# Latent attention of a hybrid diffusion block: blocks of 1024 queries, query halves in column tiles, denominators inverted in four pieces

## The reference, cut to what matters

```python
def attend(q, k, v):
    s = jnp.einsum('bqhgd,bkhd->bhgqk', q, k, preferred_element_type=jnp.float32) * (HEAD_DIM ** -0.5)
    p = jax.nn.softmax(s, axis=-1).astype(v.dtype)
    return jnp.einsum('bhgqk,bkhd->bqhgd', p, v)
```

## Time and profile before

| | |
|---|---|
| Median of three runs | 3813.49 us (3811.07 to 3816.92) |
| Profiled execution | 3814.73 us, its span 3813.1 us |
| Busy over the span | PE 93%, DVE 58%, ACT 34%, POOL 39% |
| Stage that is changed | 762 to 1894 us, 30% of the span |

### The profile page before, as it was taken

How to read it: one execution, slowest core, us unless ns; L and a number is a source line. 1 busy time by engine, 2 the same in 40 slices (tenths; PEclk the granted TensorE clock), 3 DMA queues, 4 the chain that set the end, 5 groups by cost and what they waited for, 6 DMA issues and landing times. The chain is left out here.

```text
span 3813.1 us, 51191 instructions
## 1 busy us (share of the span) xinstructions
PE 3534.7 (93%) x17340; PEld 2666.5 (70%) x17340; DVE 2207.0 (58%) x3467; ACT 1283.1 (34%) x2070; POOL 1494.8 (39%) x991
## 2 busy tenths in 40 slices
PE   6999996799999999999769959999999998999798
PEld 4787883456666666666468847888998886887586
DVE  4666644566666666666346655443334443777576
ACT  3422334334444444444320034222223332664300
POOL 1133313456777777677623321100000001444354
PEclk8999997789999999999979979999999999999899
DMA  5234537411111111111155442221211114677563
GB/s 189 95 113 131 141 94 233 132 38 34 34 34 33 39 37 33 34 34 33 44 190 176 138 136 97 78 71 66 73 57 57 47 36 131 207 220 242 210 210 137
DMA packets 313681, 394.25 MB, mean 103 GB/s; under 512 B 81965, under 2 KB 208061, under 8 KB 313361
## 3 DMA queue, kind: packets, MB, share of 16 engines
q1 hardware_dynamic: 281312, 317.34, 27.3%
q10 hardware_dynamic: 21040, 37.43, 3.1%
q0 software_dynamic: 11136, 36.98, 2.4%
HBM read 267.99 MB, written 121.20 MB: 102 GB/s over the span
## 5 line engine op out<-in xcount | busy, mean ns | idle before, releaser
L1403 DVE TENSOR_REDUCE al_mx<-al_sx 128x1 f32<-128x512 f32 (+1 forms) x960 | 562.6, 632 | 267.9 <-PE al_sx L1480 254.7
L235 PE MATMUL pj_acc<-pj_whi,pj_h_hi 128*128 128x512 f32 x1808 | 711.6, 394 | 0.0
L236 PE MATMUL pj_acc<-pj_wlo,pj_h_hi 128*128 128x512 f32 x1808 | 706.0, 390 | 0.0
L237 PE MATMUL pj_acc<-pj_whi,pj_h_lo 128*128 128x512 f32 x1808 | 705.5, 390 | 0.0
L1343 ACT ACTIVATE al_e<-al_st 128x1024 f32<-128x1024 f32 x432 | 443.2, 1027 | 577.5 <-PE al_st L1493 568.0
L845 DVE TENSOR_TENSOR pj_h_lo<-pj_hall,pj_h_hi 128x1024 fp32r<-128x1024 f32 x258 | 377.8, 1465 | 282.4 <-ACT pj_h_hi L713 282.3
L1373 POOL TENSOR_TENSOR al_acc_p<-al_acc_p,al_e 128x1024 f32<-128x1024 f32 x192 | 457.5, 2383 | 20.1 <-POOL al_acc_p L1369 0.4
L787 POOL TENSOR_TENSOR pj_wlo<-pj_wst,pj_whi 128x2048 fp32r<-128x2048 f32 x28 | 129.0, 4606 | 728.0 <-ACT pj_whi L697 728.0
L713 ACT ACTIVATE pj_h_hi<-pj_hall 128x1024 fp32r<-128x1024 f32 x258 | 270.5, 1055 | 415.2 <-PE pj_acc L237 397.4
L1502 PE MATMUL al_acc<-al_e,vres 128*64 128x512 f32 x1728 | 402.5, 601 | 0.0
L235 PEld LDWEIGHTS pj_acc<-pj_whi,pj_h_hi 128*128 128x128 f32 x1808 | 341.5, 189 | 70.1 <-issue 0.6
(11 more groups left out here) (285 smaller groups left out, 5731.8 us busy)
## 6 DMA issues: line engine op xcount, KB each, us to landing
s_proj<-pj_stage SPq DMA_DIRECT2D x162, 256.0 KB, 2.0
pj_wst<-in_w ACTq DMA_DIRECT2D x28, 1024.0 KB, 5.5
ml_k<-s_proj SPq DMA_DIRECT2D x36, 512.0 KB, 4.4
ml_v<-s_proj SPq DMA_DIRECT2D x36, 512.0 KB, 8.6
mo_in<-s_proj SPq DMA_DIRECT2D x34, 512.0 KB, 6.2
hm_w<-in_ada_w SPq DMA_DIRECT2D x16, 1024.0 KB, 8.7
ml_qt<-s_qt SPq DMA_DIRECT2D x32, 512.0 KB, 6.1
s_h<-ml_h POOLq DMA_DIRECT2D x32, 512.0 KB, 8.0
```

The costliest lines, as they stand in the source:

```text
L235: nc.tensor.matmul(out, s_hi, m_hi, start=start, stop=False)
L236: nc.tensor.matmul(out, s_hi, m_lo, start=False, stop=False)
L237: return nc.tensor.matmul(out, s_lo, m_hi, start=False, stop=stop)
L1403: V.tensor_reduce(mx[:, x:x + 1], slots[x % NSX][:, 0:spans[x % NS][1]], AX.X, ALU.max).then_inc(sx_max, 1)
```

## The change

The stage gets a function of its own, `latent_attention`, unrolled (no hardware loop). `attention` stays for the context. A block is now 1024 queries of one head; there are 24.

- Key tiles are taken singly, `NP = 18`, with the two query halves side by side: `st` holds 128 keys x 1024 queries. The two value matmuls of a step now share the value tile, and the two column tiles are the two query halves. Nothing has to be folded: `acc` holds 64 rows for each half.
- The denominators come from a matmul with `ones` of 128x64 as the stationary operand, so each arrives copied on 64 partitions, in the layout of `acc` (`denominators`, before key tile 7). ACT copies them out of PSUM into `den`. DVE inverts them in place in four pieces of 128x128 at key tiles 8 to 11, and multiplies by `ot` at tile 13 (`norm`). PE turns the product by four transposes at tile 14, and ACT copies the result out for the store.
- The sums: DVE adds tiles 0, 1, 3, 9, 10, 12, POOL all others and the two parts together. `asum` is 128x1024; the add of the two halves is gone.
- 40 maxima per block. The places 20 and 38 of the slot order are taken by the denominators and the transposes. There are three maxima before key tiles 1 and 4, and none before 16 and 17.
- The bias of the next block is done at key tile 15 of 18, and its row goes out in eight DMAs.

```diff
@@ -1562,6 +1562,333 @@
                 values(NKV - 1, n, n, 0)
                 folded(n - 1, n - 1)
                 folded(n, n)
+
+
+def latent_attention(nc, m, a, s, keep, kres, vres):
...
+    NP, HALVES = NT, 2
+    BLOCKS = LT * P // (HALVES * CH)
+    TOTAL = NQ * BLOCKS
+    W = HALVES * CH
+    QT = W // P
...
+    DEN_AT, TURN_AT, NSX = 20, 38, 3
+    AHEAD, EXTRA = (2, 3, 2, 2, 3) + (2,) * 10 + (0, 0, 0), 2
+    DEN_J, PIECES_J, ON_J, TURN_J, BIAS_J = 7, (8, 9, 10, 11), 13, 14, 15
+    ADD_D, ADD_P = (1, 3, 9, 10, 12), (5, 4, 6, 7, 8, 11, 13, 14, 15, 16, 17)
...
+    turn = [("max", x) for x in range(NX)]
+    turn.insert(DEN_AT, ("den", 0))
+    turn.insert(TURN_AT, ("turn", 0))
...
+    def items(n):
+
+        at = 0
+        out = []
+        for j in range(NP):
+            extra = EXTRA if j and j % C == 0 else 0
+            out.append((range(at, at + extra), range(at + extra, at + extra + AHEAD[j])))
+            at += extra + AHEAD[j]
...
+            def row(n):
+                sp.wait_ge(negm_done, n + 1)
+                if n == 0:
+                    sp.wait_ge(zero_done, 1)
+                for i in range(QT):
+                    sp.dma_start(qb[HD:HD + 1, n % 2, i * P:(i + 1) * P].bitcast(F32), negm[:, n % 2, i:i + 1].bitcast(F32)).then_inc(row_ld[n % 2], 16)
+
+            def store(n):
+                sp.wait_ge(o_done, n + 1)
+                for b in range(HALVES):
+                    rows = s["attn"][tokens(n), head(n) * HD:(head(n) + 1) * HD][b * CH:(b + 1) * CH]
+                    sp.dma_start(rows.rearrange("(t p) d -> p t d", p=P), o[:, n % 2, :, b, :]).then_inc(stored[n % 2], 16)
+
+            for n in range(2):
+                load_x(n)
+                load(n)
+            row(0)
+            for n in range(TOTAL):
+                if n + 2 < TOTAL:
+
+                    sp.wait_ge(sx_mm, (n + 1) * NX)
+                    load_x(n + 2)
+                if n:
+                    store(n - 1)
+                if n + 1 < TOTAL:
+                    row(n + 1)
+                if n + 2 < TOTAL:
+
+                    sp.wait_ge(st_mm, (n + 1) * NP)
+                    load(n + 2)
+            store(TOTAL - 1)
...
+            def denominators(n, slot):
+                act.wait_ge(den_mm, n + 1)
+                if n:
+                    act.wait_ge(on_done, n)
+                nc.scalar.activation(den[:], slots[slot][:], ACT.Copy).then_inc(den_out, 1)
+
+            def result(n, slot):
+                act.wait_ge(turn_mm, n + 1)
+                if n >= 2:
+                    act.wait_ge(stored[n % 2], 16 * HALVES * (n // 2))
+                nc.scalar.activation(o[:, n % 2].rearrange("p t b d -> p (t b d)"), slots[slot][:], ACT.Copy).then_inc(o_done, 1)
...
+                    if j == DEN_J and n:
+                        denominators(n - 1, DEN_AT % NSX)
+                    if j == TURN_J and n:
+                        result(n - 1, TURN_AT % NSX)
+                    weights(n, j)
...
+                if n >= 2:
+                    pool.wait_ge(den_mm, n - 1)
+                nc.gpsimd.tensor_tensor(asum[:, n % 2], acc_p[:], acc_d[:], ALU.add).then_inc(asum_done, 1)
...
+            def inverse(n, i):
+                dve.wait_ge(den_out, n + 1)
+                V.reciprocal(den[:, i * P:(i + 1) * P], den[:, i * P:(i + 1) * P]).then_inc(rden_done, 1)
+
+            def norm(n):
+                dve.wait_ge(rden_done, CH // P * (n + 1))
+                dve.wait_ge(ot_done, n + 1)
+                if n:
+                    dve.wait_ge(turn_mm, n)
+                V.tensor_tensor(on[:], ot[:, n % 2, :], den[:], ALU.mult).then_inc(on_done, 1)
...
+            adds = {3: (0,), 6: (1,), 12: (2, 3), 15: (4,)}
+            for n in range(TOTAL):
+                for j, (extra, ahead) in enumerate(items(n)):
+                    some(extra)
+                    for i in adds.get(j, ()):
+                        add(n, i)
+                    if j == ON_J and n:
+                        norm(n - 1)
+                    some(ahead)
+                    if j in PIECES_J and n:
+                        inverse(n - 1, PIECES_J.index(j))
+                    if j == BIAS_J and n + 1 < TOTAL:
+                        bias(n + 1)
+            for i in range(CH // P):
+                inverse(TOTAL - 1, i)
+            norm(TOTAL - 1)
...
+                for b in range(HALVES):
+                    cols = slice(b * CH, (b + 1) * CH)
+                    mm(st[k % 2][:, b], kres[:, g, keys], qa[:, p, cols], start=True, stop=False)
+                    y = mm(st[k % 2][:, b], kres[:, NKV + g, keys], qb[:, p, cols], start=False, stop=True)
+                y.then_inc(st_mm, 1)
...
+                for b in range(HALVES):
+                    y = mm(acc[b * HD:(b + 1) * HD], vres[:, j, group_of(n), :], e[:, k % RING, b], start=(j == 0), stop=(j == NP - 1))
+                y.then_inc(pv_mm, 1)
...
+                for b in range(HALVES):
+                    y = mm(slots[slot][b * HD:(b + 1) * HD], ones[:], asum[:, n % 2, b], start=True, stop=True)
+                y.then_inc(den_mm, 1)
...
+                for i in range(CH // P):
+                    y = nc.tensor.transpose(slots[slot][:, i * P:(i + 1) * P], on[:, i * P:(i + 1) * P], keep["ident"][:])
+                y.then_inc(turn_mm, 1)
...
+                    if j == 0 and n:
+                        for i in range(NP - C, NP):
+                            values(n - 1, i)
+                    if j and j % C == 0:
+                        some(extra)
+                        for i in range(j - C, j):
+                            values(n, i)
+                    some(ahead)
+                    scores(n, j)
...
@@ -2372,7 +2699,7 @@
     m.end()
     attention(nc, m, a, s, keep, kres, vres, "ac_", 0, CT, 1, CT)
     m.end()
-    attention(nc, m, a, s, keep, kres, vres, "al_", CT, 4, LT // 4, NT)
+    latent_attention(nc, m, a, s, keep, kres, vres)
     m.end()
     attention_stack.close()
     out_weights = OutWeights(nc, m, 0, a["w_out0"], 2)
```

175 lines of the change are left out of this document (added).

## The result

The changed kernel takes 3865.13 us (median of 4, 3863.35 to 3867.61) against 3814.71 us before (median of 4, 3811.07 to 3816.92): 1.0128 times as long, 95% interval 1.0115 to 1.0141. The forecast was 3851 us. The span of the profiled execution grew by 51.1 us, from 3813.1 to 3864.2 us. Of that, 43.5 us lie before the end of the stage (1894.4 to 1937.8 us) and 7.6 us after it, in code that the change does not touch.

What follows compares the result with a forecast made beforehand. PE was taken as the bound, busy 1100.9 of 1102.9 us. A block: 43.97 + 2.3 + 0.46 + 0.3 + 0.1 = 47.1 us against 45.96; with the stage's ends +38, so 3813.5 + 38 = 3851 us, range 3795 to 3885.

Steps and rivals of the forecast that it cites:

- PE's own work and the small waits: Per 1024 queries: PE's work falls from 45.96 to 43.97 us; waits 0.46 (tile 17), 0.3 (slots, place 41), 0.1 (bias row).
- The reciprocal: DVE's inversion of 128x128, four per block: 0.94 us each, from a slope of 6 ns per column.
- The race: Key tiles 8 to 13: DVE needs 15.8 us, PE 13.6, so PE waits 2.3 us per block for maxima.
- place 37: Matmul in the slot order at key tile 13, waiting for the maximum of place 34: a 1.5 us wait.
- DVE's hole: After place 25 the next matmul for DVE comes only after the values: about 1.5 us no order can use.
- POOL's hold: At key tile 12 DVE's adds stand until POOL's add of tile 11 ends: about 0.65 us.
- B: Rival: DVE keeps up if a reciprocal costs 0.3 us; block 44.6, 3794 us; chance 0.18.
- C: Rival: waits half as large, smaller hole or holds; block 45.6 to 46.0, 3817 to 3826, down to 3806; chance 0.12.
- rival D: DVE meets POOL's full 2.4 us at tile 12 (3892), or is passed over before the row (3906); chance 0.15.
- The row: Next block's bias row, eight DMAs on SP: there 9.7 us after place 41, PE at 9.6; costs 0.1 us.
- The scores of tile 17: No maxima between tiles 15, 16, 17, so these scores wait for the exponentials of 15: 0.46 us.
- The ends of the stage: First scores at 793.0 us, last values end at 1917.3, stage end at 1932.3 against 1894.4: +38 us.

Runs made afterwards that it cites:

- DVE out of the way: Changed kernel with each reciprocal on 1 column and POOL's running adds on 128 of 1024 columns, work left out: 3802.5 us, a block of 45.07.
- The first experiment, the small reciprocals: Changed kernel with each of the four reciprocals per block on 1 column instead of 128: 3854.6 us, ratio 1.0104.
- the ninth DMA: Changed kernel with one more DMA of 128 values ahead of the eight of the bias row: 3877.9 us, ratio 1.0162.
- the version with the transposes there: The swapped and late version with transposes between the scores of tiles 16 and 17: 3962.4 us; with bias ahead of add and row ahead of stores, 3795.5.
- the swapped and late version: Changed kernel, POOL adding tile 9 and DVE tile 11, reciprocals and product behind the bias, transposes in the next block: 3813.2 us, ratio 1.0000.

## Why the prediction was right, and where not

**PE's own work and the small waits.** Summed without the race they were 43.97 + 0.46 + 0.3 + 0.1 = 44.83 us. Measured with DVE out of the way: 45.07, or 45.0 without the long first block. Right to 0.2 us. The transposes cost 0.44 instead of 0.5 us (0.35 from 1304.16 to 1304.51, 0.09 behind them). The pass of ones cost 1.21 instead of 1.11 (1.01 in the lines below, 0.20 around it); I had it at the price of a pair of value matmuls. What is left of the 0.2 us I can't place.

```profile
1332.14 1.08 PE L1856 MATMUL al_sx<-al_asum,al_ones 128*64 128x512 f32 x4
1333.15 0.50 PE L1827 MATMUL al_sx<-kres,al_qx 128*128 128x512 f32 x1
```

**The reciprocal.** 943 ns against 0.94 us: the slope of the earlier trace rows carried over from 4 columns to 128. The estimate of about 1.2 us that I had made from the Trainium skill ("VectorE: DVE Perf Modes", First, the fixed hardware budget) does not hold here: 943 ns were measured, and the 25 us that hung on it did not come.

**The race.** Forecast: PE waits 2.3 us, in two small pieces at tiles 11 and 12 and 1.5 us at place 37. Measured: 0.3, 0.3 and 1.5 us. By the experiments 2.33 us per block. From place 22 to place 37 PE took 15.80 us (1334.41 to 1350.21), as forecast, and DVE's hole was 1.63 us against 1.5. POOL's hold was 0.7 us against 0.65, but that was partly luck. I gave no working for it and said that POOL had just begun on tile 11; in fact it was 1.6 us into an add of 2.35 us.

**What failed: rivals B and C.** I said that with a reciprocal of 0.3 us the race would be PE's, a block 44.6 us and the time 3794 us, and that the sign turns at 0.46 us. The first experiment took the reciprocals away almost wholly and came to 3855 us. I had counted the hold as a constant of 0.65 us. It depends on when DVE comes: late, it meets the last 0.7 us of POOL's add; in time, it meets 2.0 us of it. That is rival D's mechanism, which I had priced as a case of its own, while it stands behind B: a cheap reciprocal would have led into D. So the chances of faster were too high for B's reason.

**The row.** Said to cost 0.1 us; it had about 0.15 us of slack. The sentence that each further hold would go straight into it was nearly right, as the ninth DMA shows (0.51 us for 0.66).

**The scores of tile 17.** 0.46 us, as the earlier trace rows had them; the version with the transposes there shows that it could be filled.

**The ends of the stage.** First scores 794.3 us against 793.0. The first scores of the last block come at 1884.3 against 1879.7: 1.3 from the start and 3.3 from the blocks. These are 0.2 longer (47.31 between two waits at place 37, 1302.90 and 1350.21, against 47.1), 4.8 us in 23 blocks, while the first one holds 1.9 us above the usual instead of 3.4. The last values end at 1923.2 against 1917.3; the last block took 1.3 us more. There, without maxima, DVE's two adds took 6.15 us where 2.4 is their work, and the transposes waited 0.92 us for the product behind them. From there on it took 14.6 us against 15.0. The stage ends 43.5 us later instead of 38.

**After the stage.** I had put the rest at no change. It takes 7.6 us more (1918.7 to 1926.4 us). It is not one place: up to the first of four marks in the later stages the same code takes 1.0 us more, and from mark to mark and to the end 3.0, 0.0, 2.8 and 0.9. All twelve other kernels built on the changed one show it too, with 1922.7 to 1927.1 us. I have no run that tells why, so this is left open. It also moves the sign, which I had turning at a block of 45.45 us: the swapped and late version has 45.07 and a ratio of 1.0000. By the profiled executions the forecast was 13 us short, 5.5 in the stage and 7.6 behind it.

## What to carry to other kernels

When two engines share the work by turns, ask at each meeting when each of them arrives, and price a hold by the arrival and not by a mean: here a delay of 3.5 us and a hold of 2 us covered each other, each removed alone gained 0.3 to 0.7 us of 2.3, and only a version without both showed what they cost. Put an instruction into the stretch where the engine has nothing urgent, even if it is held there, rather than shorten it in a tight one. And when a step moves, follow its DMA too: with two stores ahead of a row on SP a change that should gain lost about 145 us, and with the stores behind the row it gave the fastest kernel.

## What the runs showed of the hardware

DVE's adds, with two operands in SBUF, stood until POOL's running add had ended, from wherever they fell into it: two adds take 2.4 us alone, 3.15 when POOL has 0.74 us left, and 4.44 when it has 2.03 left. The product `on` takes 0.68 us alone and 1.89 with POOL at work. Maxima out of PSUM and reciprocals, with one operand, were not held: two maxima took 1.29 us under POOL's train at 1339.49, as in the earlier trace rows, and four reciprocals ran in 3.37 us in the middle of POOL's train from 1324.21 to 1337.76 us in the swapped and late version. I had known the hold from the earlier trace rows, but not that the reciprocal is free of it; this is what made the late place possible.

A reciprocal goes by columns: 0.15 us for 1 column, 0.94 for 128, 3.34 for 512. That is 6.2 ns per column and 0.14 us fixed, and four of 128 in a queue took 3.37. So dividing it in four cost nothing in itself.

After PE had stood 5.73 us, the granted clock was 0.52 over the next 4.5 us, near the lower of its two levels (1.2 and 2.4 GHz), and 1.00 after that. After waits of 1.32 us in the changed kernel and 1.70 us with the small reciprocals it stayed at 1.00.
